# Weighted output rows kept in their PSUM banks at the stage boundaries, and row squares spread between weight roundings, in a one-core decoder layer

## What is computed

```
def rmsnorm(x, g):
    y = x * rsqrt(mean(x * x, axis=-1) + RMS_EPS)
    return y * g

f = swiglu(rmsnorm(h, ffn1_g_pre), ffn1_w_gu, ffn1_w_down)
h = h + 0.5 * rmsnorm(f, ffn1_g_post)
m = hybrid_mixer(rmsnorm(h, mix_g_pre), ...)
h = h + rmsnorm(m, mix_g_post)
c = memory_cross_attention(rmsnorm(h, mem_g_pre), rmsnorm(mem, mem_g_kv), w_mq, w_mkv, w_mo)
h = h + rmsnorm(c, mem_g_post)
f = swiglu(rmsnorm(h, ffn2_g_pre), ffn2_w_gu, ffn2_w_down)
h = h + 0.5 * rmsnorm(f, ffn2_g_post)
```

## Time and profile before

| | before |
|---|---|
| median of 3 runs | 1203.12 us (1202.19 to 1206.01) |
| the profiled execution, its time | 1202.4 us |
| its span, first to last instruction | 1200.7 us |
| PE busy | 1162.8 us, 97% of the span |
| PEld / POOL / ACT / DVE busy | 963.0 / 472.7 / 445.9 / 355.6 us |
| mean granted clock of PE | 0.994 |

### The profile page before, as it was taken

One profiled execution on the slowest core, in us unless ns is written; L12 is line 12 of the kernel. 1 busy time (PEld: TensorE's weight loads), 2 busy tenths in 40 slices (PEclk: granted clock), 3 DMA queues, 4 the chain that ended last, 5 costly groups with the idle time before them and its releaser, 6 DMA issues.

```text
span 1200.7 us, 14983 instructions
## 1 busy us (share of the span) xinstructions
PE 1162.8 (97%) x5565; PEld 963.0 (80%) x5565; DVE 355.6 (30%) x713; ACT 445.9 (37%) x728; POOL 472.7 (39%) x216
## 2 busy tenths in 40 slices
PE   8999999999999999999899999799999999999998
PEld 6888888888888778788678878678888888888886
DVE  3131221310006264655546104516213122130003
ACT  5232232322126455454535534425523223232213
POOL 2344354354442542222224753122543434435441
PEclk9999999999999999999999999899999999999999
DMA  6232323232322222111223442022332333323233
GB/s 197 88 105 87 105 87 105 88 105 88 105 90 69 88 88 71 53 53 54 71 70 117 146 142 88 18 71 71 93 101 94 98 97 95 100 93 104 90 102 109
DMA packets 83835, 110.91 MB, mean 92 GB/s; under 512 B 8718, under 2 KB 53836, under 8 KB 83788
## 3 DMA queue, kind: packets, MB, share of 16 engines
q1 hardware_dynamic: 83696, 110.24, 28.1%
q10 hardware_dynamic: 92, 0.02, 0.0%
HBM read 108.14 MB, written 2.10 MB: 92 GB/s over the span
## 4 chain that ended last, share of the span: by engine, by line
PE 67%; issue 19%; POOL 8%; DVE 4%; ACT 1%; DMA 1%; SPq 0%; POOLq 0%; DVEq 0%; ACTq 0%
PE bank L1397 22%; PE bank L1401 22%; PE bank L1398 22%; POOL w_lo L566 7%; DVE h L1050 1%; DVE tmp L1039 1%; DMA raw<-in_ffn_w_gu 1%; ACT w_hi L622 0%; POOL q_hi L604 0%; POOL q_lo L604 0%; DVE pt_lo L1170 0%; DVE xl L1002 0%; PE bank L1418 0%; PE bank L1421 0%; DVE smax L1144 0%
## 5 line engine op out<-in xcount | busy, mean ns | idle before, releaser
L566 POOL TENSOR_TENSOR w_lo<-raw,w_hi 128x1024 fp32r<-128x1024 f32 x193 | 461.5, 2403 | 707.5 <-ACT w_hi L622 695.2
L1397 PE MATMUL bank<-xh,w_hi 128*128 128x512 f32 (+1 forms) x920 | 353.3, 384 | 5.2 <-POOL w_lo L566 2.6
L1401 PE MATMUL bank<-xl,w_hi 128*128 128x512 f32 (+1 forms) x920 | 351.8, 382 | 0.0
L1398 PE MATMUL bank<-xh,w_lo 128*128 128x512 f32 (+1 forms) x920 | 351.7, 382 | 0.0
L622 ACT ACTIVATE w_hi<-raw 128x1024 fp32r<-128x1024 f32 x196 | 204.5, 1056 | 361.3 <-DMA raw<-in_ffn_w_down 169.3
L1397 PEld LDWEIGHTS bank<-xh,w_hi 128*128 128x128 f32 x920 | 173.0, 188 | 40.3 <-issue 3.9
L1401 PEld LDWEIGHTS bank<-xl,w_hi 128*128 128x128 f32 x920 | 173.1, 188 | 33.9
L1398 PEld LDWEIGHTS bank<-xh,w_lo 128*128 128x128 f32 x920 | 173.2, 188 | 32.2
L1397 PE MATMUL bank<-w_hi,mid_hi 128*128 128x512 f32 x352 | 137.3, 390 | 0.0
L1398 PE MATMUL bank<-w_hi,mid_lo 128*128 128x512 f32 x352 | 137.0, 389 | 0.0
L1401 PE MATMUL bank<-w_lo,mid_hi 128*128 128x512 f32 x352 | 137.0, 389 | 0.0
(11 more groups left out here) (227 smaller groups left out, 1168.6 us busy)
## 6 DMA issues: line engine op xcount, KB each, us to landing
raw<-in_ffn_w_gu SPq DMA_DIRECT2D x176, 256.0 KB, 2.9
raw<-in_ffn_w_down SPq DMA_DIRECT2D x88, 256.0 KB, 2.8
raw<-in_mix_w_in SPq DMA_DIRECT2D x48, 256.0 KB, 2.8
raw<-in_mem_w_kv SPq DMA_DIRECT2D x32, 256.0 KB, 3.1
raw<-in_mix_w_out SPq DMA_DIRECT2D x16, 256.0 KB, 2.8
raw<-in_mem_w_q SPq DMA_DIRECT2D x16, 256.0 KB, 3.0
raw<-in_mem_w_o SPq DMA_DIRECT2D x16, 256.0 KB, 2.9
h<-in_x SPq DMA_DIRECT2D x4, 512.0 KB, 5.3
```

Of the source, the lines that this page charges most:

```text
L566: gp.tensor_tensor(w_lo[:, n % SLOTS, :], raw[:, n % SLOTS, :], w_hi[:, n % SLOTS, :].bitcast(F32), ALU.subtract).then_inc(lo_ready, 1)
L1397: pe.matmul(dst, w[0], x[0], start=start, stop=False, skip_group_check=loose)
L1398: pe.matmul(dst, w[1], x[0], start=False, stop=False, skip_group_check=loose)
L1401: return pe.matmul(dst, w[0], x[1], start=False, stop=stop, skip_group_check=loose)
```

## The change

Three things change, on ACT, DVE and PE's waits; no arithmetic is added.

1. `weigh` writes its product back into the bank that it read, and `rows` reads it there, for all eight tiles of boundaries 0 and 2 and for tiles 0 to 3 of boundary 1. Tiles 4 to 7 of boundary 1 and the whole of boundary 3 stay in `tmp`. PE's first key block, which overwrites banks 4 to 7, now waits for `finished` in place of `weighted`.
2. At boundaries 0 and 2 block start + 4 is rounded between the second and the third square.
3. In the memory stage the four squares leave their places behind the keys. Three go behind the roundings up to the three q blocks, the last ahead of `pre_root(2)`.

```diff
@@ rows_norm on ACT (s = 0 and 2)
                     for t in range(TC):
                         pre_square(s + 1, t)
+                        if t == 1:
+                            round_to(start + 5)
@@ memory on ACT
                                        ACT.Copy, scale=MEM_D ** -0.5).then_inc(kv_h, 1)
-                    pre_square(2, 2 * g)
-                    pre_square(2, 2 * g + 1)
                 for k in range(3):
                     round_to(mem_block("q", 0, k) + 1)
+                    pre_square(2, k)
                 for g in range(2):
...
                     round_to((mem_block("q", 0, KB - 1), mem_block("q", 1, 0))[g] + 1)
+                pre_square(2, 3)
                 pre_root(2)
@@ rows_norm on DVE
+                def weighted_at(n):
+                    return out_bank(s, n) if s in (0, 2) or s == 1 and n < 4 else tmp[:, n % 4, :]
+
...
-                    dve.scalar_tensor_tensor(out=tmp[:, n % 4, :], in0=out_bank(s, n)[:, :], scalar=POST_SCALE[s],
+                    dve.scalar_tensor_tensor(out=weighted_at(n)[:, :], in0=out_bank(s, n)[:, :], scalar=POST_SCALE[s],
...
-                        dve.scalar_tensor_tensor(out=h[:, t, cols], in0=tmp[:, n % 4, :], scalar=f_rinv[:, r],
+                        dve.scalar_tensor_tensor(out=h[:, t, cols], in0=weighted_at(n)[:, :], scalar=f_rinv[:, r],
@@ memory on PE
-                            free = {m: (xl_ready, x_count(2, 2 * m + 1)) if g else (weighted, ROWS + m + 1)
+                            free = {m: (xl_ready, x_count(2, 2 * m + 1)) if g else (finished, ROWS + m + 1)
```

## The result

| | before | after |
|---|---|---|
| median | 1203.18 us (1202.19 to 1206.01, 4 runs) | 1195.23 us (1193.14 to 1197.21, 4 runs) |
| ratio, 95% interval | | 0.9931 (0.9909 to 0.9952) |
| profiled execution, time and span | 1202.4, 1200.7 us | 1197.21, 1195.5 us |
| mean granted clock of PE in it | 0.994 | 0.994 |

The forecast was 1194.9 us. The median is 0.3 us from it, and the change is faster by 0.7%. The total is right while three of its terms are not.

A forecast was written before the change was run, and what follows sets the result against it. PE, busy for 97% of the span, was taken as the bound, so edits gain only what PE waits. Terms 2.0 + 2.0 + 1.2 + 3.0 = 8.2 us gave 1203.1 - 8.2 = 1194.9 us, range 1190.5 to 1199.5.

The forecast's parts named there:

- rival (b): Residual steps stay stalled because h is read and written in SBUF; only 3.0 us gained, 1200.1 us; chance 0.05.
- Edit 1, boundaries 0 and 2: Weighted rows in banks end the residual step's stall beside POOL's split; 2.0 us at each boundary.
- the sentence on what is late next: At boundary 0, `xl` has its first chunks at 376.3, PE needs it about 376.8; gain nearly whole.
- A sign that I had named as right: PE's waits for the residual step L1050 and for `xl` would be gone.
- Edit 1, boundary 1: Ending the stall at 642.00 removes PE's wait for the eighth weighing; 1.2 us; the pair at 649.76 stalls still.
- The price of the bank: Residual steps with weighted rows in a bank; price taken as 0, bounded between -0.07 and +0.2 us each.
- Rival (d): In-place bank writes at the boundaries are dear; total gain zero at 0.29 us more per step; chance 0.03.
- Edit 3: Moving the memory stage's squares ends PE's waits for B_KV + 6 and B_KV + 10; 3.0 us, ends 1.5 and 3.9.
- (e): More than the sum: B_KV + 17's wait goes, 1194.0 us, or a low-clock stretch, 1191 to 1192; chance 0.17.
- rival (a): The memory stage is bound by landings, leaving 0 to 1.5 us there; 1196.4 to 1197.9 us; chance 0.12.
- Edit 2: Block start + 4 rounded earlier at boundaries 0 and 2; price and gain 0.
- The clock: PE's low-clock stretch in 755 to 760 may go or gain a second; up to 3 us either way.

The follow-up runs named there:

- one_input_sum: The changed kernel with the sum into f_ms taking one column as a scalar pointer, so one SBUF tensor input; 1194.37 us, ratio 0.9931.
- one_input_again: The changed kernel with one column of the f_ms sum as a scalar pointer, run beside the changed kernel on one chip; 1192.99 us, ratio 0.9916.
- squares_only: The kernel before with only the four squares of the memory stage moved; 1200.1 us, ratio 0.9975.
- memsets_later: The kernel of one_input_again with POOL's clears of q_hi and q_lo behind the splits of B_IN + 3 to 5; 1193.12 us, ratio 0.9913.
- split_earlier: The kernel before with ACT's rounding of block start + 2 behind the first root, not the second; 1202.89 us, ratio 0.9996.

## Why the prediction was right, and where it was not

- **What bounds it, and what stalls: right.** The pair of SBUF inputs was the cause. The rival (b), that the bank doesn't free the step, is out: twenty steps on a bank took 752 ns at most, the one at boundary 0 that ran through a split (the second of the pair at 372.02) among them.
- **Edit 1, boundaries 0 and 2: a miss.** The term was 2.0 us each with ends of 1.5 and 2.2, and 1.20 and 1.21 came. The failed step is the sentence on what is late next. It let DVE come 2.17 us earlier, as if L1050 alone could be held by the split. Two instructions behind the pair in the same queue stood a sum with two SBUF inputs; it is in the order lists that I had made of the change. It now pays 1.14 - 0.15 = 0.99 us, and 2.17 - 0.99 = 1.18 is left of DVE's gain, close to what came. one_input_sum and one_input_again, which take one of the two inputs away, gave 2.02 to 2.05 at each. A sign that I had named as right failed with it: PE's wait for `xl` isn't gone, 0.57 us of it is left at boundary 0 and 0.59 at boundary 2.
- **Edit 1, boundary 1: right in size** (1.2, and 1.20). I had said that the last pair stalls still; it didn't, since the split that had held it now waits for a landing. Nobody waited for it.
- **The price of the bank: right.** Zero was taken, within -0.07 and +0.2. The write cost 0.009 us and the read gained 0.002 (747 against 749 ns). Of the two estimates weighed there, the one from the Trainium skill (Perfetto Trace Analysis, "Optimizing Scalar/DVE Operations"), by which an access of VectorE costs about 125 ns on PSUM in place of about 60, was not borne out for these forms, where the output or one of two inputs went over to a bank. Rival (d) needed 0.29 us a step.
- **Edit 3: right in mechanism, and a fraction low.** The term was 3.0 with ends of 1.5 and 3.9; 3.80 and 3.98 came, and 4.35 in squares_only. Both waits that I had priced went. What varied was the third, for B_KV + 17. From issue to rounding its loads took 5.39 us before, 5.32 in memsets_later (wait 0.77), 4.80 after (0.27), and 3.63 in squares_only (none). I had left this third wait in; the case without it, (e), was the better description. In one_input_again it was nil, but of the two waits that I had priced the second, for B_KV + 10, came back with 0.48 us: its block was rounded 5.21 us after the issue (667.26 to 672.47), waiting for the landing, where my working had 3.5 and a cover of 0.6. That is what I had named as the low end, one landing late, and a small piece of rival (a). (The chain of 3.5, 0.25, 1.06 and 2.4 in that working adds up to 7.2 and not 7.3; nothing hangs on it.) With the third wait nearly whole, in memsets_later, the term reads 2.86.
- **Edit 2: right**, nothing.
- **The clock.** I had allowed up to 3 us either way. The attention's segment ran from -2.28 to +1.61 us over the executions shown, as its clock in 740 to 785 ran from 1.00 to 0.89. Over the nine runs of the changed kernel, the three with a mean clock of 0.998 or more took 1193.14, 1194.10 and 1195.19 us, and the six with 0.994 or 0.995 took 1195.83 to 1197.21.
- **The sum.** 2.0 + 2.0 + 1.2 + 3.0 = 8.2 was forecast, and 1.20 + 1.21 + 1.20 + 3.80 = 7.4 came: 1.6 too much at the boundaries, 0.8 too little in the memory stage. The medians show 7.95 and, in the second series, 7.7. Two errors in opposite directions made the total look better than its parts.

## What to carry to other kernels

When a stall goes that comes from a shared resource, walk down the queue of the engine that was held and look at every instruction that stands in the same stretch for the same property, however small it is: here an addition of two columns cost 1 us. What decided here was the kind of its inputs (two in SBUF, against one and a bank or a pointer), so list all two-input forms beside the neighbour's splits before costing the edit. And where runs spread by 4 us, compare segments of the trace between fixed instructions: 1.2 us at a boundary repeats within 0.02 there, and one run of an edit that does nothing can show 3.

## What the runs showed of the hardware that was not expected

- A one-column VectorE addition with two SBUF inputs waited for the end of GpSimd's split: 1147 ns in place of 153, and 1.69 us at boundary 2 of split_earlier. With a scalar pointer as the second operand it took 199 to 215 ns everywhere.
- It goes the other way too: GpSimd's split took 2.81 us in place of 2.40 when it began beside a residual step with two SBUF inputs (once, at boundary 2 of split_earlier).
- VectorE's writes to a bank took 692 ns against 683 to SBUF for 128 x 512.
- The same kernel had its clock lowered in one stretch of the memory attention in some executions and in none of it in others. Before that stretch PE had gone on working with gaps (row below: the window ahead of the first low one in the changed kernel, busy for 2.69 of 5 us at full clock). Why one execution keeps the clock and the next doesn't wasn't tried and stays open; the edits here aren't shown to have an effect on it.

```profile
745.00:750.00 5.00, 2.69 (x17) 2.14 (x15) 3.57 (x9) 2.78 (x7) 0.00 (x0) 1.00 0.00 0
```
